# Column sums of the gated recurrence's weights: ones-matmuls per key block against block adds on GpSimd and one matmul per direction

## What is computed

```python
def step(carry, inp):
    ...
    dmat = bcum[..., :, None] - bcum[..., None, :] + it[..., None, :]
    dmat = jnp.where(lower, dmat, -jnp.inf)
    ...
    s_qk = jnp.einsum('bhld,bhsd->bhls', qt, kt) * w_intra
    num = w_inter[..., None] * jnp.einsum('bhld,bhde->bhle', qt, C) + jnp.einsum('bhls,bhse->bhle', s_qk, vt)
    den = w_inter * jnp.einsum('bhld,bhd->bhl', qt, n) + jnp.sum(s_qk, axis=-1)
    h_out = num / jnp.maximum(jnp.abs(den), jnp.exp(-m_t))[..., None]
```

## Time and profile before

| | |
|---|---|
| median of 3 runs | 3412.16 us (3408.64 to 3413.48) |
| the profiled execution | 3410.6 us, its span 3409.3 us |
| TensorE busy | 3318.4 us (97%), mean granted clock 0.994 |
| VectorE, ScalarE, GpSimd busy | 1514.2, 1394.3, 1409.7 us (44%, 41%, 41%) |
| mean busy share of DMA engines by hardware queue 1 | 25.7% |
| the chain that ended last | 91% TensorE, 4% VectorE, 3% ScalarE |

### The profile page before, as it was taken

The page is one execution under the profiler, slowest core; times in us unless marked ns, Lnnn a source line. Parts: engine busy times, 40 slices in busy tenths (PEclk is TensorE's granted clock), DMA queues, the critical chain, the costliest instruction groups (busy, mean ns, idle before and its releaser), DMA issues.

```text
span 3409.3 us, 39050 instructions
## 1 busy us (share of the span) xinstructions
PE 3318.4 (97%) x14310; PEld 2544.9 (75%) x14310; DVE 1514.2 (44%) x2792; ACT 1394.3 (41%) x2610; POOL 1409.7 (41%) x1052
## 2 busy tenths in 40 slices
PE   8999999999999999999999999998999999899999
PEld 6667776878888667777688888864788887478887
DVE  5544566343534444456634464456322234632222
ACT  3543435433323354344534333456433335643322
POOL 2233333445554323333245555541355444135554
PEclk9999999999999999999999999999999999999999
DMA  4122121233332212212123333210233331023333
GB/s 141 62 84 68 62 68 59 86 106 112 97 96 94 65 58 66 66 62 68 56 93 112 119 97 99 90 62 19 79 111 96 96 95 63 25 68 108 98 97 100
DMA packets 155077, 281.96 MB, mean 83 GB/s; under 512 B 19172, under 2 KB 20965, under 8 KB 154886
## 3 DMA queue, kind: packets, MB, share of 16 engines
q1 hardware_dynamic: 154598, 279.39, 25.7%
q10 hardware_dynamic: 288, 0.07, 0.0%
HBM read 276.62 MB, written 2.77 MB: 82 GB/s over the span
## 4 chain that ended last, share of the span: by engine, by line
PE 91%; DVE 4%; ACT 3%; DMA 1%; issue 1%; SPq 0%; POOL 0%; DVEq 0%; ACTq 0%; POOLq 0%
PE bank L543 26%; PE bank L545 26%; PE bank L544 26%; PE bank L601 3%; PE bank L610 2%; PE bank L774 1%; PE bank L788 1%; PE bank L786 1%; PE bank L909 1%; PE bank L575 1%; PE bank L731 1%; PE bank L653 1%; PE bank L835 1%; PE bank L901 1%; DMA raw<-in_units 0%
## 5 line engine op out<-in xcount | busy, mean ns | idle before, releaser
L2110 POOL TENSOR_TENSOR wl<-raw,wh 128x512 fp32r<-128x512 f32 x1012 | 1378.9, 1369 | 1984.5 <-ACT wh L978 1961.6
L543 PE MATMUL bank<-Uh,wh 128*128 128x512 f32 x2720 | 1120.9, 412 | 9.9 <-DVE Ul L1430 7.7
L545 PE MATMUL bank<-Uh,wl 128*128 128x512 f32 x2720 | 1065.7, 392 | 0.0
L978 ACT ACTIVATE wh<-raw 128x512 fp32r<-128x512 f32 x1012 | 624.9, 626 | 1075.1 <-PE bank L545 1049.6
L544 PE MATMUL bank<-Ul,wh 128*128 128x512 f32 x2720 | 1063.4, 391 | 0.0
L543 PEld LDWEIGHTS bank<-Uh,wh 128*128 128x128 f32 x2720 | 513.9, 189 | 163.8 <-issue 47.1
L544 PEld LDWEIGHTS bank<-Ul,wh 128*128 128x128 f32 x2720 | 514.1, 189 | 122.3 <-issue 18.4
L545 PEld LDWEIGHTS bank<-Uh,wl 128*128 128x128 f32 x2720 | 512.8, 189 | 110.7
L1419 DVE TENSOR_TENSOR work<-bank,rs 128x512 f32<-128x512 f32 x308 | 212.6, 690 | 776.6 <-PE bank L545 736.2
L543 PE MATMUL bank<-Hh,wh 128*128 128x512 f32 x1258 | 504.7, 401 | 4.4 <-DVE small L1692 1.9
L545 PE MATMUL bank<-Hh,wl 128*128 128x512 f32 x1258 | 490.3, 390 | 0.0
(11 more groups left out here) (231 smaller groups left out, 2724.7 us busy)
## 6 DMA issues: line engine op xcount, KB each, us to landing
raw<-in_units SPq DMA_DIRECT2D x1012, 256.0 KB, 2.7
xT<-in_xT SPq DMA_DIRECT2D x8, 256.0 KB, 5.3
out<-xT SPq DMA_DIRECT2D x8, 256.0 KB, 2.8
table<-scratch SPq DMA_DIRECT2D x16, 112.0 KB, 3.1
work<-in_dft SPq DMA_DIRECT2D x2, 512.0 KB
work<-in_counts SPq DMA_DIRECT2D x2, 512.0 KB, 5.0
table<-scratch SPq DMA_DIRECT2D x48, 16.0 KB, 2.5
const<-in_const SPq DMA_DIRECT2D x1, 576.0 KB, 7.4
```

Source lines behind the costliest of these rows:

```text
L543: nc.tensor.matmul(out, H, xh, start=k == 0, stop=False)
L545: mm = nc.tensor.matmul(out, L, xh, start=False, stop=k == x.kt - 1)
L978: nc.scalar.activation(g.wh[:, a:a + PK * P], g.raw[:, a:a + PK * P], ACT.Copy).then_inc(s_hi, 1)
L2110: nc.gpsimd.tensor_tensor(g.wl[:, a:a + PK * P], g.raw[:, a:a + PK * P], g.wh[:, a:a + PK * P].bitcast(F32), ALU.subtract).then_inc(g.s_lo, 1)
```

## The change

For each head and direction GpSimd now adds the weight tiles of the four key blocks into one tile `acc`. The first item of a direction is copied without its diagonal block, and the later items are added over their whole width, which never reaches that first diagonal block. TensorE sums that first diagonal block alone, with a 128-column matmul by ones right behind line 786 of the first item, and `acc` (384 columns) with one matmul by ones at the end of the head, after a wait for GpSimd. ScalarE waits for GpSimd too before it refills a weight tile. In `sums_of` the copy of `NUM[d]` comes first, and the absolute value of `DEN[d]` after its new wait. `acc` lies in tiles that are free at that time; two new waits on VectorE guard their next use. GpSimd's adds are put into its stream of low halves four pieces behind the place where TensorE stands after the item's three K steps.

```diff
+    def scan_sums(self, h, d):
+
+        return self.w(((25, 26), (13, 14))[h == 3][d]), ((P, S), (0, S - P))[d]
@@ TensorE, the head's loop over x
-                    nc.tensor.matmul(bank[NUM[d]][:, lo:hi], vt[:, src * P:(src + 1) * P], wt[:, lo:hi],
-                                     start=n_ == 0, stop=n_ == NT - 1)
-                    nc.tensor.matmul(bank[DEN[d]][:, lo:hi], c("ones"), wt[:, lo:hi], start=n_ == 0,
-                                     stop=n_ == NT - 1).then_inc(s_pe, T("wv", i, h, x - 1))
+                    mm = nc.tensor.matmul(bank[NUM[d]][:, lo:hi], vt[:, src * P:(src + 1) * P], wt[:, lo:hi],
+                                          start=n_ == 0, stop=n_ == NT - 1)
+                    if n_ == 0:
+                        a = src * P
+                        mm = nc.tensor.matmul(bank[DEN[d]][:, a:a + P], c("ones"), wt[:, a:a + P], start=True, stop=True)
+                    mm.then_inc(s_pe, T("wv", i, h, x - 1))
...
+            for d in range(2):
+                acc, (lo, hi) = g.scan_sums(h, d)
+                pe.wait_ge(g.s_pool, at("G", "sums", i, h, 6 + d))
+                nc.tensor.matmul(bank[DEN[d]][:, lo:hi], c("ones"), acc[:, lo:hi], start=True, stop=True).then_inc(
+                    s_pe, T("den", i, h, d))
@@ ScalarE, weights_of and sums_of
             if x >= 4:
                 act.wait_ge(s_pe, at("T", "wv", i, h, x - 4))
+                act.wait_ge(g.s_pool, at("G", "sums", i, h, x - 4))
             elif h:
                 act.wait_ge(s_pe, at("T", "wv", i, h - 1, x + 4))
+                act.wait_ge(g.s_pool, at("G", "sums", i, h - 1, x + 4))
...
                 act.wait_ge(s_pe, at("T", "wv", i, h, 6 + d))
+                nc.scalar.activation(w(23 + d), bank[NUM[d]][:, :], ACT.Copy).then_inc(s_act, C("num", i, h, d))
                 if h:
                     act.wait_ge(s_dve, at("V", "H", i, 2, h - 1))
+                act.wait_ge(s_pe, at("T", "den", i, h, d))
                 nc.scalar.activation(w(2 + d), bank[DEN[d]][:, :], ACT.Abs).then_inc(s_act, C("den", i, h, d))
-                nc.scalar.activation(w(23 + d), bank[NUM[d]][:, :], ACT.Copy).then_inc(s_act, C("num", i, h, d))
@@ GpSimd
+    def sums(i, h, x):
...
+        pool.wait_ge(g.s_dve, at("V", "wt", i, h, x))
+        if n:
+            pool.wait_ge(s_pool, G.n)
+            nc.gpsimd.tensor_tensor(acc[:, lo:hi], acc[:, lo:hi], wt[:, lo:hi], ALU.add).then_inc(
+                s_pool, G("sums", i, h, x))
+            return
...
+        nc.gpsimd.tensor_copy(acc[:, first:end], wt[:, first:end]).then_inc(s_pool, G("sums", i, h, x))
...
+                between.setdefault(g.new[("Bp", i, "scan", h, x, 0)] + RING, []).append((sums, (i, h, x)))
```

More of the change, by code:

```diff
@@ L1607, in follow @@
                 scale = {"ck": P ** -0.5, "dq": HQ ** -0.5}.get(kind)
+                if kind == "dq" and t == 1:
+                    dve.wait_ge(s_pe, at("T", "den", i, 2, 1))
                 if kind == "co" and t >= 2:
@@ L1988, in layer1 @@
         beat(i, "D", 1)
+        dve.wait_ge(s_pe, at("T", "den", i, 3, 1))
         values(i, "d0", 2, g.diff_tiles(0)[2])
@@ L2130, in pooled @@
         nc.gpsimd.tensor_tensor(out, out, u, ALU.subtract).then_inc(s_pool, G("pool", i, n))
-    at_piece = {g.product(i, "u", n).at[-1][0] + RING + 1: (i, n) for i in range(DEPTH, 2 * DEPTH) for n in range(2)}
+    def sums(i, h, x):
+        n, d, src, lo, hi = g.scan_items()[x]
+        acc, (first, end) = g.scan_sums(h, d)
+        wt = w(WEIGHT_TILES[x % 4])
+        pool.wait_ge(g.s_dve, at("V", "wt", i, h, x))
[4 more added lines that the diff above has]
+            return
+        if h:
+            pool.wait_ge(g.s_pe, at("T", "den", i, h - 1, d))
+        else:
+            pool.wait_ge(g.s_dve, at("V", "gel", i))
+        nc.gpsimd.tensor_copy(acc[:, first:end], wt[:, first:end]).then_inc(s_pool, G("sums", i, h, x))
+    between = {}
+    for i in range(DEPTH):
+        for h in range(4):
+            for x in range(8):
+                between.setdefault(g.new[("Bp", i, "scan", h, x, 0)] + RING, []).append((sums, (i, h, x)))
+    for i in range(DEPTH, 2 * DEPTH):
+        for n in range(2):
+            between.setdefault(g.product(i, "u", n).at[-1][0] + RING + 1, []).append((pooled, (i, n)))
     for p in range(len(g.pieces)):
-        if p in at_piece:
-            pooled(*at_piece[p])
+        for work, which in between.get(p, ()):
+            work(*which)
         split_weights(p)
```

## The result

The changed kernel takes 3388.78 us (median of 4 runs, 3387.14 to 3389.38), beside 3412.82 us for the kernel before: ratio 0.9929, 95% interval 0.9916 to 0.9942. That is 24.2 us less, between 20 and 29. The forecast was 31.9 us less, 3381 us; the range (3375 to 3396) holds the result.

What follows compares the result with a forecast made beforehand. TensorE, busy 97% of the span, was taken to bound the kernel; 20.6 us off its list, 6.2 from passages between heads and 5.1 from the clock sum to 31.9 us less, forecast 3381 us, range 3375 to 3396.

Steps and rivals of the forecast that it cites:

- The list: TensorE's sums by ones in the heads: 1.29 us less per direction of a head, 20.6 us in all.
- The passages: Between heads: TensorE's waits on ScalarE shrink and the new sums largely fill gaps, 6.2 us gained over two layers.
- GpSimd: In the heads: about 5.5 us more GpSimd work per head stays hidden, without new TensorE waits of note.
- The worked-out 6 us: In the heads: time free on GpSimd before a late low half makes TensorE wait.
- VectorE against GpSimd: Where heads 1 and 2 end: adds could delay VectorE's subtract; 0 in the sum, 2.2 us kept for the range.
- The clock: Behind the long gaps between heads: no lower clock level follows once they shrink, 5.1 us gained (ends 0 and 5.1).
- the first: Passages between heads: list gets shorter but gaps and clock falls stay, 20.6 us alone, 3391 us; chance 0.24.
- Rivals 2 and 4: 2: GpSimd last at head ends, 3400 us, chance 0.08; 4: a later stage bound by another engine, 3412, 0.02.
- rival 3: At head starts: GpSimd's adds wait for VectorE, low halves queue behind, TensorE starves; 3420 us, chance 0.03.

Runs made afterwards that it cites:

- the two multiples: Changed kernel with four, then ten, idle GpSimd copies ahead of each add: 3386.6 us (ratio 0.9925) and 3565.04 us (1.0450).
- ten copies: Changed kernel with ten idle GpSimd copies of the same width ahead of each add: 3565.04 us, ratio 1.0450.
- the adds alone: Kernel before, TensorE's list and ScalarE's order kept, with GpSimd's 64 adds made and not used: 3418.83 us, ratio 1.0013.

## Why the prediction was right, and where it was off

*The list.* Right, and a little smaller than put: 20.6 us were put, and the heads and what left the passages give 19.0. Most sums came off at what the chain showed, the second one of 512 and both of 384 columns 0.03 us short of it. Head 3 is 0.4 us longer than the others: with line 788 gone, TensorE comes to the last scores of the head before ScalarE has read the mean out of the same bank (the weight load of line 778 waits 0.5 us for line 1003). This wait was not foreseen; it costs 0.8 us in all.

*The passages.* Right in mechanism and size. 6.2 us were put and 6.7 came; the table gives 1.25 us longer at the first passage (1.27 put), 0.8 to 1.2 shorter at the second (0.7 put), 0.4 shorter at the third (0.4). The second was better than put in layer 1, because VectorE's low half took 0.69 us there and not 1.50. That is luck and not the absence of an add: a low half of the weights on GpSimd ended 0.14 us into it. In layer 2 VectorE's low half took 1.46 us, and the passage 16.29, as put. That the sums fall into a gap is shown twice: left out, they save 6.2 us and not 10.3, and moved ahead of what the third passage follows they make it 1.3 us longer.

*GpSimd.* Right: no wait of TensorE or ScalarE for it is in the lists beyond the one at the start, and there is room for 2 us more per item of 384 columns. The worked-out 6 us hold within what the two multiples tell.

*VectorE against GpSimd.* The 2.2 us kept for the range were not needed: no add met that subtract. But what a meeting costs was misread. The 0.96 us that the 1.50 was held against is a mean over hindered and free ones; a free one takes 0.69 us. In the earlier trace rows the subtract met not an add but a low half of the weights, and it ended 0.55 us behind it. So it is at other places; the first pair is the kernel before from head 2 to 3, the second the changed kernel in layer 2 from head 1 to 2:

```profile
413.32 1.33 POOL L2110 TENSOR_TENSOR wl<-raw,wh 128x512 fp32r<-128x512 f32 x1 [1.49 <-ACT wh L978]
414.20 1.00 DVE L1428 TENSOR_TENSOR Hl<-work,Hh 128x512 fp32r<-128x512 f32 x1 [0.70 <-ACT Hh L1009]
...
1438.84 2.52 POOL L2127 TENSOR_TENSOR wl<-raw,wh 128x512 fp32r<-128x512 f32 x2 [2.61 <-ACT wh L989]
1440.46 1.46 DVE L1442 TENSOR_TENSOR Hl<-work,Hh 128x512 fp32r<-128x512 f32 x1 [2.95 <-ACT Hh L1020]
```

GpSimd's end is 414.65 and 1441.36, VectorE's 415.20 and 1441.92. Of the 110 subtracts of this form in each kernel 92 began while GpSimd was in an instruction. All 92 of the kernel before and 91 of the changed one ended 0.55 us (0.546 to 0.554) behind GpSimd's instruction; the one left is that at 358.28, which had only 0.14 us to wait. A subtract of the kernel before with its first input in PSUM (at 44.44) began 1.2 us before GpSimd's end and took 0.69 all the same. The Trainium skill's page "SBUF — State Buffer", section "Who interferes with whom", calls what the two share an exclusive lock and says that a VectorE instruction with two SBUF inputs contends with a GpSimd instruction that reads SBUF; these rows agree. So a meeting costs what is left of the other's instruction less 0.14 us: 0.8 us in the earlier trace rows, where the prediction read 0.54. For an add of 384 columns, 1.01 us when free, it could be up to 0.87 (an estimate from these rows).

*The clock.* This is the step that failed: 5.1 us were put for it, and nothing of it came in the whole time. In the passages it was right: the granted clock is 1.00 behind all six, and from the first item to the first scores the two layers took 428.7 us in the first profile of the kernel before and 398.1 in that of the changed kernel, 30.6 less, where 31.9 were put. But the gain was counted as a gain of the whole. The profiled span fell by 21.2 us, so 9.4 were lost elsewhere. Outside the recurrences the low clock cost 15.5 us before and 27.5 after, at the start of the program, behind the first scores of both layers (2.04 us of gap in both kernels, 1.00 before and 0.79 after) and in the second kind of layer, where no instruction was changed:

```profile
476.00:484.00 8.00, 7.87 (x26) 5.05 (x26) 2.41 (x11) 2.81 (x7) 1.93 (x2) 0.79 0.14 40
...
2196.00:2204.00 8.00, 6.06 (x22) 4.42 (x22) 6.90 (x17) 2.03 (x8) 1.38 (x2) 0.79 0.11 33
```

The timed executions say the same without a profile. In 48 of the kernel before the mean granted clock is 0.9927, which is 25.0 us of 3413.6; in nine of the changed kernel it is 0.9922, 26.4 us of 3388.6. The means differ by 25.0 us, and the list and the passages at full clock give 25.7. Between the recurrences nothing changed: with the low clock taken out, the stretch from the first scores of layer 1 to the recurrence of layer 2 took 875.8 to 876.8 us in every profile but that with ten copies.

The clock term should have been taken at its lower end, 0, with the range as it stood. Then the forecast is 3386, 3 us from the measured time and not 8. Three falls seen in one execution are a draw; and even though such falls came behind 9 of 12 long gaps in all, and none behind what is left of them in the changed kernel, the loss over the program did not get smaller. Why it stays is open. Of the rivals, the first gave 3391, nearer to the measured time than the forecast; that it is not what happened is told by the traces alone: the gaps are gone. Rivals 2 and 4 are out by the list of waits, and rival 3 needs some 2 to 5 us more per item than there is.

## What to carry to other kernels

Where one engine's list sets the time, an operation that can be deferred is best put where that engine waits anyway, and it then costs only what is longer than the gap; find out first what the wait follows, since ahead of that point the same work costs all of its time. Of a gap read from a trace count the gap itself, and keep the low clock behind it for the range: here it was often there, it left with the gap, and the loss of the whole program stayed. The mean granted clock of all timed executions tells whether a few microseconds are the edit or the clock. Before a mean duration is used as an undisturbed one, look at the single instructions. Compare kernels of a few microseconds' difference stretch by stretch between fixed instructions: that repeated to 0.03 us here, while the whole time moved by 10.

## What the runs showed of the hardware

The low granted clock of one core costs between 18 and 32 us of 3400 in these profiles (about 84 us with ten copies), in pieces of about 1.7 us. In the three profiles that have TensorE's list of before and in the first of the changed kernel, each piece between the program's start and its end followed a gap that the trace puts at 1.6 us or more, while other gaps of 1.5 to 2.6 us were followed by none. An unchanged program had the pieces in other places in its second profile. In the three profiles with the list of before (the kernel before twice, and the adds alone), the lower level came behind 9 of 12 long gaps before the gate spreads and behind 2 of 6 gaps before the first scores.

A VectorE subtract over two SBUF tiles that begins during a GpSimd instruction ended 0.55 us behind that instruction, in 183 of 184 cases, and takes 0.69 us alone. GpSimd's adds of 384 columns took 1.01 us, and 1.45 where they began during such a VectorE instruction; those of 128 columns mostly 0.46 and 0.64; the 16 of 256 columns 0.73. Its copy of 384 columns takes 0.51 us, half of the free add.
